# Hybrid decoder layer: where three output merges stand on VectorE, and how 15 row steps are spread over the stages of fronts 1 and 2

## The reference, cut to what matters

```python
proj = h @ w_in[i]
pool_in, z, xbc, dt_raw, g_pool, g_ssm = jnp.split(proj, SPLITS, axis=-1)
a_out = pool_mixer(pool_in, pool_w[i], pool_scale[i])
m_out = ssm_mixer(z, xbc, dt_raw, ...)           # ends in  y @ ssm_out
merged = jax.nn.sigmoid(g_pool) * a_out + jax.nn.sigmoid(g_ssm) * m_out
h = layer_norm(DN_ALPHA * h + merged @ w_out[i], ln1_g[i], ln1_b[i])
h = layer_norm(DN_ALPHA * h + peer(h, w_q[i], sub_keys[i], expert_u[i], expert_v[i]), ...)
# peer, per token: top 16 experts of each of 8 heads, then
#   h = x . expert_u[e];  act = gelu(h) * gate;  out = sum act * expert_v[e]
```

## Time and profile before

| | |
|---|---|
| median of 3 runs | 3664.77 us (3661.15 to 3666.88) |
| the profiled execution's own time | 3671.08 us |
| its span, first to last instruction | 3669.3 us |
| TensorE (PE) busy | 2878.5 us, 78% |
| VectorE (DVE) busy | 2693.3 us, 73% |
| GpSimd (POOL) busy | 2066.5 us, 56% |
| ScalarE (ACT) busy | 1044.7 us, 28% |
| moved by DMA | 1394.94 MB, of which the gathers (queue 0) 1073.86 MB and the weights' queue 313.42 MB |

### The profile page before, as it was taken

The page is one execution under the profiler, slowest core; times in us unless marked ns, Lnnn a source line. Parts: engine busy times, 40 slices in busy tenths (PEclk is TensorE's granted clock), DMA queues, the critical chain, the costliest instruction groups (busy, mean ns, idle before and its releaser), DMA issues.

```text
span 3669.3 us, 46078 instructions
## 1 busy us (share of the span) xinstructions
PE 2878.5 (78%) x16012; PEld 2048.4 (56%) x16012; DVE 2693.3 (73%) x5768; ACT 1044.7 (28%) x2692; POOL 2066.5 (56%) x1839
## 2 busy tenths in 40 slices
PE   8987988788889879999978879999977853443443
PEld 7886877677777437777765427877754410000000
DVE  3318756999975788777766887777776886668767
ACT  5512532343321213444312114444212110001000
POOL 0003433566664667766656676767657676555553
PEclk9988999899989889999989879999988866555555
DMA  6558999999999999999999999999999999999997
GB/s 245 209 223 312 374 364 383 361 369 393 387 340 357 411 409 401 406 408 405 393 400 399 410 403 408 408 401 393 407 381 412 400 400 412 421 421 421 421 421 315
DMA packets 316566, 1394.94 MB, mean 380 GB/s; under 512 B 35376, under 2 KB 40880, under 8 KB 251824
## 3 DMA queue, kind: packets, MB, share of 16 engines
q0 software_dynamic: 262656, 1073.86, 73.6%
q1 hardware_dynamic: 52384, 313.42, 21.6%
q10 hardware_dynamic: 1296, 4.72, 0.3%
HBM read 1387.66 MB, written 4.19 MB: 379 GB/s over the span
## 4 chain that ended last, share of the span: by engine, by line
DMA 26%; PE 22%; POOL 12%; DVE 6%; issue 5%; DVEq 1%; ACT 1%; POOLq 0%; ACTq 0%
DMA rowbuf<-ev,idx 9%; POOL rowbuf L605 9%; PE main L648 8%; DMA rowbuf<-euv,idx 4%; PE vbank L736 3%; DMA ring<-euv,idx 3%; PE main L656 2%; PE main L867 2%; PE main L852 2%; DMA rowbuf<-eu,idx 2%; DMA merged<-euv,idx 2%; DVE acc L1711 2%; DMA xT<-euv,idx 2%; PE turn L719 2%; DVE rowbuf L1685 1%
## 5 line engine op out<-in xcount | busy, mean ns | idle before, releaser
L605 POOL DMA_INDIRECT rowbuf<-eu,idx x722 | 840.1, 1164 | 809.6 <-DVE hdot L1685 288.9
L605 POOL DMA_INDIRECT rowbuf<-ev,idx x717 | 779.5, 1087 | 404.4 <-issue 191.7
L1685 DVE CUSTOM_DVE_ANT_0 rowbuf<-rowbuf,hb 128x1024 f32<-128x1024 f32 x637 | 778.6, 1224 | 161.9 <-DMA rowbuf<-eu,idx 92.8
L648 PE MATMUL main<-xT,ring 128*128 128x256 f32 (+1 forms) x4480 | 807.1, 341 | 13.9 <-DMA ring<-wblocks 10.6
L648 PEld LDWEIGHTS main<-xT,ring 128*128 128x128 f32 x4480 | 721.6, 193 | 99.6 <-issue 29.4
L736 PE MATMUL vbank<-rowbuf,vdiag 64*64 64x512 f32 x2992 | 502.2, 770 | 257.5 <-DMA rowbuf<-ev,idx 130.1
L1711 DVE SCALAR_TENSOR_TENSOR acc<-rowbuf,hact,acc 128x1024 f32<-128x1024 f32 x427 | 549.6, 1287 | 94.1 <-DMA rowbuf<-ev,idx 84.6
L736 PEld LDWEIGHTS vbank<-rowbuf,vdiag 64*64 64x64 f32 x2992 | 105.3, 157 | 573.8 <-ACT vdiag L1077 331.8
L1077 ACT ACTIVATE vdiag<-spots,hact 128x64 f32<-128x64 f32 x531 | 168.2, 343 | 565.2 <-DVE hact L1694 352.5
L852 PE MATMUL main<-late,ring 128*128 128x256 f32 (+1 forms) x1280 | 240.4, 352 | 39.4 <-issue 28.7
L852 PEld LDWEIGHTS main<-late,ring 128*128 128x128 f32 x1280 | 214.2, 202 | 65.0 <-issue 32.6
(11 more groups left out here) (249 smaller groups left out, 3818.3 us busy)
## 6 DMA issues: line engine op xcount, KB each, us to landing
ring<-wblocks SPq DMA_DIRECT2D x280, 1024.0 KB, 8.1
rowbuf<-eu,idx POOLq DMA_INDIRECT x722, 12.9
rowbuf<-ev,idx POOLq DMA_INDIRECT x717, 13.1
pw<-poolw SPq DMA_DIRECT2D x20, 256.0 KB, 9.6
h_out<-acc ACTq DMA_DIRECT2D x8, 512.0 KB
xT<-xt SPq DMA_DIRECT2D x3, 1024.0 KB, 12.7
zy<-x SPq DMA_DIRECT2D x3, 1024.0 KB, 13.6
craw_ln<-ln1g SPq DMA_DIRECT2D x5, 512.0 KB, 15.0
```

What stands on the lines that cost most here:

```text
L605: pool.indirect_dma_start(rows[r], None, (eu, ev)[table], bass.IndirectOffsetOnAxis(ap=idx[c % 2][:, u, k:k + 1], axis=0)).then_inc(row_re ...
L648: last = pe.matmul(dst_[:, ct * tc:(ct + 1) * tc], w[:, k, ct * P:(ct + 1) * P], src[:, k, 0:tc], start=(k == 0), stop=(k == KD - 1))
L1685: last = dve.tensor_tensor_reduce(r, r, h, 1.0, 0.0, ALU.mult, ALU.add, hdot[:, g % 2, k:k + 1])
```

## The change

First, `WIDTHS` of fronts 1 and 2, as (groups, outputs, W, D, D) in steps. The sums, and so the begins of all fronts, stay as they are.

Second, the merges of q = 0, 1, 2 stand 3 of 7 offsets later in VectorE's order, in all fronts; that of q = 3 stays.

```diff
-WIDTHS = ((128, 28, 16, 42, 8), (40, 6, 5, 10, 9), (104, 20, 12, 34, 32), (124, 26, 16, 40, 38), (128, 28, 16, 42, 42))
+WIDTHS = ((128, 28, 16, 42, 8), (31, 13, 7, 10, 9), (98, 25, 13, 34, 32), (124, 26, 16, 40, 38), (128, 28, 16, 42, 42))
...
                 o = place(c, ATC)
                 for q in range(4):
-                    until(o(q * PC + PC - 1))
-                    weave(o(q * PC + PC), front_pair(c, q), 1)
+                    at_ = q * PC + PC + (3 if q < 3 else 0)
+                    until(o(at_ - 1))
+                    weave(o(at_), front_pair(c, q), 1)
```

## The result

The changed kernel takes 3678.38 us, median of 6 runs (3675.2 to 3681.8), beside 3665.69 us, median of 6 (3661.15 to 3669.2), of the kernel before: ratio 1.0034, 95% interval 1.0021 to 1.0046. It is slower by 12.7 us, outside the range and on the side of rival C.

The account below looks back on a forecast made before the run. The prediction took DMA traffic as the bound, with only the engines' rest to win: front 1 -0.6 and front 2 -5.5, together -6.1 us from the median 3664.77, giving 3659 us; range 3647 to 3674.

Parts of the forecast that it names:

- rival C: Weights come late in front 1's and 2's outputs, groups give nothing: slower by 10.6 up to 20 us; chance 0.20.
- Front 1, groups, -11.5 us: Front 1's groups, nine steps fewer, get 11.5 us shorter, held by a floor of 40.23 us per group.
- First ... 2.4: Front 1's first group, 43.08 us against the 40.23 floor, gets 2.4 us shorter with one dot fewer before its pooling.
- Fourth ... I take 3: Front 1's fourth group gains 3 of 4.3 us over the floor, as VectorE's rows fall from 10 to 8 steps.
- Front 1, outputs, ... taken +9.2 us: Front 1's outputs, seven steps more, become bound by DMA with 2.5 us of rest left: 9.2 us longer.
- The clock was priced at 0: In the new outputs, PE's slower clock after waits for weights is hidden behind DMA: 0 us.
- Front 1, W, +1.7: Front 1's W, two steps more and 2 us of rest left, becomes 1.7 us longer.
- Front 2, groups, -13.6: Front 2's groups, nearly full in VectorE and DMA, lose six steps: 3.4 us a group, 13.6 us shorter.
- Row shares ... 2 sums of 1.29 off VectorE, within the above, 0: 533 instead of 531 ev rows go to PE, taking two sums off VectorE: 0 us extra.
- Front 2, outputs, +10.1; W, -2: Front 2's outputs, five steps more, get 10.1 us longer; its W, one step more but less rest, 2 shorter.
- The merges themselves: Later merges in all fronts let 1 to 3 steps of rows pass first; by themselves 0 us.
- Behind 1270 us nothing changes: After front 2 the kernel stays the same and every us carries to the end, as DMA rests little there.

Follow-up runs that it names:

- e4: Kernel before with the later merges and only front 2's six steps moved, front 1's steps as before: 3666.53 us, ratio 0.9995.
- e7: Changed kernel with far fewer row steps in the groups, front 1 16 (28 in outputs), front 2 68 (55 in outputs): one run, 3730.67 us.
- e5: Changed kernel with one ScalarE gelu (rows 16 to 31) at step 36 instead of 34: 3678.22 us, ratio 1.0023.
- e6: Changed kernel with 24 or 32 useless PE matmuls ahead of each second product of front 1's outputs: 3676.38 us, ratio 1.0019.
- e14: Kernel before with front 1's new widths alone, front 2's steps and all merges as before: 3683.48 us, ratio 1.0039.
- e1: Kernel before with the new widths of fronts 1 and 2 alone, merges in their old places: 3675.57 us, ratio 1.0019.
- e3: Kernel before with the later merges and only front 1's nine steps moved, front 2's steps as before: 3686.35 us, ratio 1.0044.
- e2: Kernel before with the later merges alone, all row steps as before: 3667.80 us, ratio 0.9995.
- e8: Changed kernel with only three of front 1's nine steps moved, 37 steps in its groups: 3671.86 us, ratio 1.0011.

## Why the prediction was wrong, step by step

**"Front 1, groups, -11.5 us": failed.** Measured from the first pooling matmul to the first output, 155.85 us before and 151.65 after: -4.2. The third group gave 5.6 of the 6.1 (up to 3.3 of them come without the change, as e4 shows), and the second became 0.9 longer. "First ... 2.4" gave nothing: I had taken what stood over the floor for rows. The pitch is 42.3 even with 16 steps (e7), so at most 0.8 of it was rows; the group begins after a wait of 16.01 us, and its pooling matmuls take 2.04 us instead of 1.06. "Fourth ... I take 3" gave nothing either (26.25 to 26.60), but there the reading was right: with the gelu out of the way it is 23.15 (e5), 3.1 us less. The rows left, and a gelu with two table loads took their place. The step that failed is that every us over a floor was priced as rows, and that nothing was asked about what comes next in the queues.

**"Front 1, outputs, ... taken +9.2 us": too low** (and the 9.2 lay outside the "+7.5 to +9" of its own heading). Measured from the first output's L648 to W, 63.42 and 76.18 us: +12.8. The mechanism was right (share 1.01, and 4.0 us of rest against the 2.5 that I had left). Of the 12.8, 3.5 lie ahead of the first product, where a dot and a sum stand ahead of what ScalarE and PE wait for, and 9.2 behind it. The clock was priced at 0 "since per output PE needs about 12 us and DMA 17, so it is hidden"; e6 shows that 3.0 us were not. That it is more than PE's clock is argued from the order alone: a late product frees its ring slot later, so that the next block is asked for later too.

**"Front 1, W, +1.7": +3.1** (126.8 to 129.9 from W to front 2's first pooling). The sum for front 1 is +11.6 where I had -0.6, and that is nearly all of the loss in medians.

**"Front 2, groups, -13.6": failed.** From the first pooling to the first product, 372.5 and 373.9 us: +1.4. What six steps fewer give is seen between kernels with the same front 1. With 31 steps there it is 378.7 (e14) to 370.0 (e1) and 378.3 (e3) to 373.9 (changed), 8.7 and 4.5 us; with 40 steps it is nothing, 369.7 (e2) to 369.8 (e4). So the price of 3.4 us a group was too high in all three pairs. With 40 steps the third group lost its row ahead of L698 with the change of front 2's steps (91.2 to 95.4 us); with 31 steps it had none in either kernel. And front 1's steps by themselves cost front 2 6.2 us (372.5 to 378.7, before to e14). The step that failed there is **"Row shares ... 2 sums of 1.29 off VectorE, within the above, 0"**: I counted how many rows go to PE and not which.

**"Front 2, outputs, +10.1; W, -2": the wrong way round.** Outputs went from 87.5 to 85.4, and W to the next front from 281.7 to 285.5. The outputs' windows moved 388 GB/s before and 396 after, W's first 50 us 322 and 408: the outputs were nearly full before the change. Of the five steps' 5.2 MB they took 1.2 (33.9 to 35.1 MB), and the traffic ran on behind them, where the stretch from W to the next front moved 115.9 MB instead of 110.2. Front 2 in all is +3.1 where I had -5.5.

**"The merges themselves": 0, and 0 it is** with old steps (e2, 0.9995), within what can be told. The cover of a front 3 sigmoid held: front 3 shows no stall of L1531 and became no longer (796.1 to 788.4 us from its first pooling matmul to front 4's).

**"Behind 1270 us nothing changes": not so.** Front 3's outputs take 89.7 us instead of 97.9, at the same full rate, and move 37.1 MB instead of 40.4. The seven kernels with 31 and 98 steps have 89.7 to 92.2 us there; those with other steps in front 1 or 2 have 92.7 to 98.2, but for e7 (89.8). About 4 us of this, on the average, are left at front 4. The sum took no term for it; its cause stays open.

**The rivals.** C holds. Its point of decision, groups of fronts 1 and 2 together shorter by less than 11 us, is met with 2.8. Its price, 10.6 us upwards, was of the right size. Its mechanism is right in part: late blocks and slow restarts stretch front 1's outputs, but front 2's were not stretched, PE's waits before front 1's four products are 17.5 us and not over 20, and what it didn't name, the shift of PE's rows, the gelu and the pair ahead of L1505, stands in the groups and the first output. Its "alone it needs 2.6" for a block stands in no row; it is 1 MB at 411 GB/s. In front 0's groups of the trace of before, where no rows are gathered, a block takes 4.8 us (median) from issue to landing. I had put 0.2 on it against 0.45 on a forecast that rested on every us over a floor being rows.

## What to carry to other kernels

Time over a floor is not yet time of the work that one means to move: before such a step is priced, read in each group what its longest wait is for, and what stands next in the queue when the moved work has gone. Where an order is planned by shares or a running remainder, a change in one stage moves single pieces in all later ones; print the plan of both versions and compare it at the points where an engine waits, since one row a step later went with 3 us more for a group here. And try both directions: the change, with nine steps moved out of front 1's groups, lost 0.34%, and three steps the other way won 0.33% with the later merges and nothing without them.

## What the runs showed of the hardware that was not expected

- A wait of PE of 1.95 to 6.36 us ahead of a product went with 9.0 to 10.3 us instead of 7.38; one of 3.67 us in e1 did not, and one of 2.62 in e8 did (8.86). The length of the last wait alone doesn't tell: ahead of the 1.95 us PE had already stood for 3.89. With matmuls without use in the wait's place (e6) all four took 7.3 to 7.4 us.
- A gelu of 0.21 us holds ScalarE for 2.82 us, from 471.58 to 474.40, with two table loads of 1.28 us. The Trainium skill, page ScalarE: Activation LUTs, section What ACT_TABLE_LOAD costs, gives about 2.66 us for each switch, drain included; here the gelu starts 0.02 us behind its load and the load itself 0.02 us behind the instruction before, so a switch costs 1.3 us, and the measurement decides.
- Front 0 takes 305.2 to 310.6 us in the profiled executions of kernels that don't differ there. Two profiles of such a kernel can't be compared by their ends to better than some 5 us.
